# Rotary scores of eight heads: from 128-row matmuls against a zero-padded key to 64-row matmuls in pairs

## The reference, cut to what matters

```
q = (rmsnorm(q_c) @ w_uq).reshape(b, s, 8, 128 + 64)      # per head: 128 plain and 64 rotary features
q_rope = apply_rope(q[..., 128:], cos, sin)
k_rope = apply_rope(k_r, cos, sin)                        # 64 features, shared by all heads
s = (einsum('bqhd,bkhd->bhqk', q_nope, k_nope) + einsum('bqhd,bkd->bhqk', q_rope, k_rope)) * scale
pr = softmax(where(mask, s, -1e30))
o = einsum('bhqk,bkhd->bqhd', pr, v)                      # in two query blocks of 128, keys up to the block's end
```

## Time and profile before

| | |
|---|---|
| time, median of 3 runs | 1918.1 us (1918.04 to 1918.73) |
| span of the profiled execution | 1916.0 us |
| the run's time outside the span (median less span) | 2.1 us |
| PE busy | 1895.8 us (99%) |
| PEld busy | 1686.2 us (88%) |
| DVE busy | 1449.3 us (76%) |
| ACT busy | 1101.8 us (58%) |

### The profile page before, as it was taken

The page is one execution under the profiler, slowest core; times in us unless marked ns, Lnnn a source line. Parts: engine busy times, 40 slices in busy tenths (PEclk is TensorE's granted clock), DMA queues, the critical chain, the costliest instruction groups (busy, mean ns, idle before and its releaser), DMA issues.

```text
span 1916.0 us, 30776 instructions
## 1 busy us (share of the span) xinstructions
PE 1895.8 (99%) x12030; PEld 1686.2 (88%) x12036; DVE 1449.3 (76%) x1907; ACT 1101.8 (58%) x1455; POOL 49.0 (3%) x61
## 2 busy tenths in 40 slices
PE   9999999999999999999999999999999999999998
PEld 7888999998889888999998888989888898688887
DVE  6875777677767776686777776785799988858997
ACT  6654545565546655444546554644677754756775
POOL 0000000000000000000000000000010001301000
PEclk9999999999999999999999999999999999999999
DMA  7665555356565556565455565543599855037993
GB/s 288 196 193 192 185 191 196 111 174 199 182 199 182 192 191 198 176 191 185 132 184 174 193 197 176 194 137 110 206 388 373 308 177 174 24 133 306 377 375 148
DMA packets 89682, 388.31 MB, mean 203 GB/s; under 512 B 10096, under 2 KB 10096, under 8 KB 74832
## 3 DMA queue, kind: packets, MB, share of 16 engines
q1 hardware_dynamic: 88992, 383.87, 58.4%
q0 software_dynamic: 560, 2.60, 0.3%
HBM read 385.38 MB, written 1.05 MB: 202 GB/s over the span
## 4 chain that ended last, share of the span: by engine, by line
PE 92%; DVE 5%; ACT 1%; DMA 1%; DVEq 1%; issue 1%; SPq 0%; POOL 0%; ACTq 0%
PE psa L1958 38%; PE psd L2064 9%; PE psa L2064 8%; PE psd L1958 7%; PE psd L2069 4%; PE psa L2116 4%; PE psd L2116 4%; PE psa L2069 4%; PE psd L2120 2%; PE psa L2120 2%; DVE w_lo L1167 1%; PE psa L2287 1%; DMA raw<-weights 1%; PE psa L2649 1%; PE psd L2680 1%; PE psd L2659 1%
## 5 line engine op out<-in xcount | busy, mean ns | idle before, releaser
L1167 DVE TENSOR_TENSOR w_lo<-raw,w_hi 128x1024 fp32r<-128x1024 f32 x496 | 588.3, 1229 | 187.6 <-ACT w_hi L771 185.5
L771 ACT ACTIVATE w_hi<-raw 128x1024 fp32r<-128x1024 f32 x250 | 263.4, 1053 | 290.7 <-PE psa L1958 164.1
L1958 PE MATMUL psa<-x_both,w_hi 128*128 128x256 f32 x1984 | 360.7, 284 | 1.1 <-DVE arena L1580 0.6
L1958 PEld LDWEIGHTS psa<-x_both,w_hi 128*128 128x128 f32 x1984 | 309.7, 192 | 2.7 <-DVE arena L1580 0.8
L1958 PE MATMUL psa<-x_both,w_lo 128*128 128x256 f32 x992 | 280.7, 283 | 0.0
L773 ACT ACTIVATE w_hi<-raw 128x1024 fp32r<-128x1024 f32 x250 | 261.3, 1045 | 3.2 <-DMA raw<-weights 3.2
L1958 PE MATMUL psa<-w_hi,slots_x 128*128 128x512 f32 x640 | 201.8, 396 | 0.7 <-DVE w_lo L1162 0.5
L1958 PEld LDWEIGHTS psa<-x_both,w_lo 128*128 128x128 f32 x992 | 190.3, 192 | 0.0
L1162 DVE TENSOR_TENSOR w_lo<-raw,w_hi 128x2048 fp32r<-128x2048 f32 x60 | 138.9, 2315 | 12.3 <-ACT w_hi L766 11.3
L1958 PEld LDWEIGHTS psa<-w_hi,slots_x 128*128 128x128 f32 x640 | 116.6, 188 | 25.6 <-DVE w_lo L1162 2.5
L1958 PE MATMUL psa<-w_lo,slots_x 128*128 128x512 f32 x320 | 125.2, 391 | 0.0
(11 more groups left out here) (416 smaller groups left out, 3403.2 us busy)
## 6 DMA issues: line engine op xcount, KB each, us to landing
raw<-weights SPq DMA_DIRECT2D x500, 512.0 KB, 4.8
raw<-weights SPq DMA_DIRECT2D x60, 1024.0 KB, 5.8
raw_y<-weights SPq DMA_DIRECT2D x36, 1024.0 KB, 6.1
x<-weights SPq DMA_DIRECT2D x18, 1024.0 KB, 5.9
h<-x_in SPq DMA_DIRECT2D x1, 1024.0 KB, 4.9
result<-h SPq DMA_DIRECT2D x2, 512.0 KB, 2.9
sml<-smalls POOLq DMA_DIRECT2D x1, 831.0 KB, 11.3
cst<-consts POOLq DMA_DIRECT2D x1, 683.5 KB, 8.8
```

The costliest lines, as they stand in the source:

```text
L771: act.activation(w_hi[:, s, UNIT_HALVES[0]], raw[:, s, UNIT_HALVES[0]], ACT.Copy).then_inc(hi_done, 1)
L1167: dve.tensor_tensor(w_lo[:, s, c], raw[:, s, c], w_hi[:, s, c], ALU.subtract).then_inc(lo_done, 1)
L1958: ins = pe.matmul(out, lhs, rhs, start=first and n == 0, stop=last and n == 2, skip_group_check=True)
```

## The change

The rotary half of a score now contracts over 64 partitions. `k_rot` is one tensor of 256 columns with the same 64 key features in both halves of the partitions. The even head's queries lie on partitions 0 to 63, the odd head's on 64 to 127, in natural feature order. Scores are issued in pairs: ahead of an even head PE writes both heads' masks, then the rotary scores of both (even, odd, even, odd), and then the plain scores of the even head. The plain scores of the odd head follow in the next step. The `settle()` of step 2 now stands ahead of the scores of head 2, since these write the bank of head 3 too. To put `q_rot` in its place DVE writes 32 partitions at a time, in eight instructions where there were four. A memset of `k_rot` on POOL at the start is gone.

```
-        k_rot = view(11276, 2, T)
+        k_rot = view(11276, T)
...
-            pool.memset(k_rot, 0.0)
...
-                    ins = dve.tensor_tensor(k_rot[r, j % 2, :], rope_a[r, 0, :], rope_a[r, 1, :], combined)
+                    to = 64 * (j % 2) + 32 * (j // 2)
+                    ins = dve.tensor_tensor(k_rot[to:to + 32, :], rope_a[r, 0, :], rope_a[r, 1, :], combined)
...
-                for to, a, b, combined in ((first, r1_cos, r2_sin, ALU.subtract), (second, r2_cos, r1_sin, ALU.add)):
-                    for e, part in enumerate((first, second)):
-                        dve.tensor_tensor(turned_q[to, :, e, :], a[part], b[part], combined)
+                for to, a, b, combined in ((0, r1_cos, r2_sin, ALU.subtract), (32, r2_cos, r1_sin, ALU.add)):
+                    for head in range(4):
+                        r, at = slice(32 * head, 32 * head + 32), 64 * (head % 2) + to
+                        dve.tensor_tensor(turned_q[at:at + 32, :, head // 2, :], a[r], b[r], combined)
...
-                def score(t):
-
-                    out = psa[:, (t + 2) % 4, 0:384]
-                    diagonal(out, mask)
+                def score_bank(t):
+                    return psa[:, (t + 2) % 4, 0:384]
+
+                def score_rotary(t):
+
+                    for u in (t, t + 1):
+                        diagonal(score_bank(u), mask)
                     for tt in range(TT):
                         keys = P * (tt + 1)
-                        terms = scores(t, tt, keys)
-                        for n, (a, b) in enumerate(terms):
-                            ins = pe.matmul(out[:, P * tt:P * tt + keys], a, b, start=False,
-                                            stop=tt == 1 and n == len(terms) - 1, skip_group_check=True)
+                        for u in (t, t + 1):
+                            a, b = scores(u, tt, keys)[1]
+                            pe.matmul(score_bank(u)[:, P * tt:P * tt + keys], a, b, start=False, stop=False,
+                                      skip_group_check=True)
+
+                def score(t):
+
+                    for tt in range(TT):
+                        keys = P * (tt + 1)
+                        a, b = scores(t, tt, keys)[0]
+                        ins = pe.matmul(score_bank(t)[:, P * tt:P * tt + keys], a, b, start=False, stop=tt == 1,
+                                        skip_group_check=True)
                     ins.then_inc(s_done, 1)
...
                 for t in range(items + 3):
+                    if t == 2:
+
+                        settle()
+                    if t < items and t % 2 == 0:
+                        score_rotary(t)
                     if t < items:
                         score(t)
-                    if t == 2:
-
-                        settle()
...
-                    return [(q_n[:, t, q], keys_n[:, t, 0:keys]),
-                            (q_rot[:, t // 2, q], k_rot[:, t % 2, 0:keys])]
+                    half = slice(64 * (t % 2), 64 * (t % 2) + 64)
+                    return [(q_n[:, t, q], keys_n[:, t, 0:keys]), (q_rot[half, t // 2, q], k_rot[half, 0:keys])]
```

## The result

The changed kernel takes 1924.19 us (median of 6 runs, 1921.63 to 1925.99) against 1918.07 us (6 runs, 1917.38 to 1918.73): a ratio of 1.0028 with a 95% interval of 1.0018 to 1.0038, slower by 3.5 to 7.3 us. The forecast was 1922.9 us and slower.

What follows compares the result with a forecast made beforehand. Attention bound by the ACT and DVE chain in every second step, PE in the others. Values 1.52 us and attention 0.88 us late, over two layers 4.8 us on 1918.1, gave 1922.9 us, range 1919.5 to 1924.7.

Steps and rivals of the forecast that it cites:

- What bounds the kernel: Attention: every second step limited by the chain through ACT and DVE's remainder, 2.86 us against 2.72 of PE work; others by PE.
- The eight writes: Ahead of the attention: eight DVE instructions for `q_rot` take 5.60 us, not 2.80, so PE starts the values 1.52 us late.
- fewer partitions do not make it shorter: DVE's `q_rot` writes: a 32-partition instruction lasts as long as a 64-partition one, 686 ns; cited 417 and 425 ns.
- The block: Attention on PE: two masks and a rotary pair take 1.27 us instead of 1.53, saving 0.26 us a pair.
- the uncovered load: First load of the 128-row plain scores after the 64-row ones: 0.10 us added, between nothing and 0.21 us.
- The order: Attention: a pair of steps grows from 5.00 to 5.51 us; weigh of head 4 at 17.60 against 16.72, 0.88 us late.
- The sum: Both layers: 2 x (1.52 + 0.88) = 4.8 us added to the span, for values and attention.
- Rival 1: Attention, odd steps: PE does not wait for the chain and keeps its 1.04 us per layer; 1919.1 us, chance 0.10.
- rival 2: Ahead of the attention: the values are not late, leaving only 2 x 0.88; 1919.9 us, chance 0.08.
- rival 3: Attention: masks and rotary pair cost 0.88 us, the switching hidden by plain scores; 1920.6 us, chance 0.09.
- rival 4: Attention: the rotary halves do not overlap, so masks and pair take 1.53 us; 1924.5 us, chance 0.07.
- Rival 5: Attention: PE's list is the whole bound, each pair's 0.65 us saving returns, 5.2 less 3.0; 1915.9 us, chance 0.04.

Runs made afterwards that it cites:

- experiment 3: The changed kernel with ACT writing `y_hi` of head t-4 ahead of the exponentials of head t; 1920.70 us, 1.0010 of the kernel before.
- experiment 1: The kernel before with `q_rot` written in eight DVE instructions of 32 partitions, scores still 128-row; 1921.51 us, 1.0012 of the kernel before.
- experiment 2: The changed kernel with DVE's eight instructions moved behind the split of the values' unit; 1920.63 us, 1.0010 of the kernel before.
- experiment 9: The kernel before, 128-row rotary scores and four DVE instructions kept, in the changed kernel's score order; 1922.16 us, 1.0016 of the kernel before.
- experiment 10: The changed kernel with DVE's eight writes behind the values' split, ACT's `y_hi` before its exponentials, and DVE's normalization before the maxima in even steps; 1915.60 us.
- experiment 7: The changed kernel with a pair's rotary scores issued even, even, odd, odd instead of even, odd, even, odd; 1923.51 us, 1.0024 of the kernel before.

## Why the prediction was right

**What bounds the kernel.** Right. The chain from head 4's scores to the weigh of head 2 was read as 2.86 us, and it is 2.85 us after the change, on a PE list that is quite different. That the wait was `o_done` held in experiment 3, against the name in the profile's row.

**The eight writes.** 1.52 us late, measured 1.48 and 1.47, and 1.50 and 1.46 where they were alone (experiment 1). The step "fewer partitions do not make it shorter" held: 682 ns. The forecast's own terms give 319.85 and not 319.88 for the start (319.7 and 0.15), so 1.49. It had nothing for the 0.09 us that PE loses behind the wait, on the way to the first mask; experiments 1 and 2 tie it to the wait.

**The block.** 1.27 us taken; the measured 1.93 from the masks to the turn is 1.17 to the first plain score and 0.76 for the plain scores, the same as 1.27 and 0.66. The 0.10 us for the uncovered load, a judgement then, is in the single records: the first two passes of the plain scores start 0.21 us apart (340.38 and 340.59), and in experiment 9, behind 128-row scores, 0.11 us (339.89 and 340.00).

The Trainium skill, "TensorEngine Tiling (Array Packing)", Key Properties, has the rule that a change of mode drains the engine. The trace agrees: PEld stands idle 0.21 us ahead of the 64-row loads and 0.33 us behind them in the changed kernel as well. The same page's Theoretical Speedup, up to 2x where the contraction is at most 64, is reached by the halves themselves and not by the block. Inside it one pass of both heads takes 0.11 us (339.74 to 339.85), as long as one pass of one head in experiment 9 (338.69 to 338.80), but the eight 64-row passes take 0.86 us with their edges, against 1.31 for eight 128-row passes there.

```profile
339.52 0.52 PEld L2291 LDWEIGHTS psa<-arena 64*128 64x128 f32 x8 [0.21 <-issue]
340.38 0.52 PEld L2299 LDWEIGHTS psa<-arena 128*128 128x128 f32 x4 [0.33 <-issue]
```

**The order.** The walk gave 9.23, 12.09, 14.74 and 17.60 us for turn 2, weigh 2, turn 4 and weigh 4. Measured were 9.22, 12.07, 14.72 and 17.57. Turn 0 was forecast at 4.83 and came at 4.75, turn 1 at 6.3 and 6.25. Turn 0 would be 4.80 in the forecast's own terms (3.91 + 0.89), which moves nothing behind it. The attention as a whole, from the first mask to the matmul behind it, is 0.86 us longer, against the 0.88 forecast.

**The size.** The sum was 4.8 us and PE's list shows 4.84. That they meet so closely is partly luck: the values and the attention were taken 0.04 and 0.02 us too long per layer, which makes up for most of the 0.09 that was not in the sum. The medians differ by 6.1 us, inside the range given. The profiled execution lost 1.8 us more than that of before to the lower clock, in the second stack. The median's extra 1.3 us has at least in part the same cause, for the mean granted clock of each run is on record. The changed kernel's three runs at 0.999 and 0.998 took 1921.63, 1921.79 and 1922.96 us. The kernel before, beside the experiments, took 1916.95 us in the mean of 13 runs at 0.999 and 1918.16 in that of 42 at 0.998: at the same clock the difference is 4.8 us. The other three runs of the changed kernel, at 0.997 and 0.996, are 5.2 to 7.0 us over before at their clock. Why they lie further off is not shown; only one execution of each kernel was profiled.

**The rivals.** Rival 1 (the chain is not what PE waits for) fell by experiment 3, rival 2 (the values are on time) by experiment 1, rivals 3 and 4 by the block's length. Rival 5, the pairs pay on PE's list, is false for this order and true once the waits for the values, for the remainder and for the normalization are gone, as experiment 10 shows.

## What to carry to other kernels

Before work is taken from an engine that is 99% busy, measure the chain of the other engines that runs beside it: here it was 2.86 us against 2.72 us of PE's work, so work moved out of its shadow cost more than the work saved. A regrouping that makes alternate steps long and short meets such a chain in the short ones; then the order within ACT's and DVE's steps decides whether the saving arrives. And DVE's instruction, split by partitions, cost its full length again (682 ns for 32 partitions, 686 for 64), on an engine whose lead was only 1.5 us.

## What was not expected of the hardware

64-row float32 matmuls on the two halves of the rows overlap even when the four records (two matmuls) of one half stand ahead of the four of the other: 0.86 us from the first to the next 128-row group in both orders (experiment 7). In experiment 7 they do not even start in the order of the list. Its list is 128, 128, 256 and 256 columns for the even head and then the same for the odd head, but four records of 128 columns start first (339.06, 339.07, 339.27 and 339.29) and then the four of 256 (339.39 to 339.62): each half goes through its own part of the list. A wait costs more than its length: a weigh behind a wait takes 0.73 us to the next group (343.99 to 344.72) and an undisturbed one 0.66 (341.46 to 342.12), and behind the wait for the values PE loses 0.09 us more. And TensorE's granted clock falls to 1.2 GHz for 3.4 or 6.8 us at one to three of four places of the second stack, near 1357, 1624, 1645 and 1717 us, in six different sets in the 13 profiled executions (the end of the span left out). From 1600.00 to 1627.13 us PE was busy for 26.77 us both in the changed kernel, where the clock then fell, and in the kernel before, where it did not (its PE is 6 us further in the same list there).
